# Four conditioning column groups computed beside the key and value stage instead of the gates stage

## The reference

```python
m_lat = [m[:, None, :] for m in adaln(c, w_ada[l], b_ada[l])]     # silu(c) @ w_ada + b_ada, six chunks of 2048
m_ctx = adaln(c_ctx, w_ada[l], b_ada[l])
hc = modulate(rms_norm(ctx, norm1_g[l]), m_ctx[0], m_ctx[1])
pc = hc @ w_in_l[:, :KV_WIDTH]                                    # KV_WIDTH = 3072
h = modulate(rms_norm(x, norm1_g[l]), m_lat[0], m_lat[1])
p = h @ w_in_l
ka, va, kb, vb = split_kv(p[..., :KV_WIDTH], k_norm_a[l], k_norm_b[l])    # keys: rms-normed per head
qa, qb, ga, gb = split_qg(p[..., KV_WIDTH:], q_norm_a[l], q_norm_b[l])
... # rope on queries and keys, attention a (16 heads, 4 kv heads), attention b (8 differential heads)
x_new = x + m_lat[2] * merge_branches(oa, ob, ga, gb, w_br_a[l], w_br_b[l], w_out[l])
```

## Time and profile before

| | us |
|---|---|
| median of 3 runs | 2924.48 (2924.23 to 2924.76) |
| profiled execution | 2922.52 |
| its span | 2920.7 |
| TensorE busy | 2862.6 |
| VectorE busy | 1964.6 |
| ScalarE busy | 1327.5 |
| mean granted TensorE clock | 0.993 of full speed |

### The profile page before, as it was taken

How to read it: one execution, slowest core, us unless ns; L and a number is a source line. 1 busy time by engine, 2 the same in 40 slices (tenths; PEclk the granted TensorE clock), 3 DMA queues, 4 the chain that set the end, 5 groups by cost and what they waited for, 6 DMA issues and landing times.

```text
span 2920.7 us, 34636 instructions
## 1 busy us (share of the span) xinstructions
PE 2862.6 (98%) x13645; PEld 2367.1 (81%) x13645; DVE 1964.6 (67%) x2525; ACT 1327.5 (45%) x1651; POOL 23.5 (1%) x47
## 2 busy tenths in 40 slices
PE   7999999999999999999999999999999999999999
PEld 7888788888888887788888777788878888888887
DVE  5775599999978667753347877767766655655444
ACT  4445454444444446532334545554444444444333
POOL 2000000000000000000000000000000000000000
PEclk9999999999999999999999999999999999999999
DMA  6444577777778887533346655548756777676554
GB/s 215 144 126 145 165 245 255 250 254 258 252 244 271 271 263 234 171 101 95 93 137 188 187 173 173 174 139 260 234 183 223 224 228 226 220 226 206 190 192 151
DMA packets 299954, 583.23 MB, mean 200 GB/s; under 512 B 18393, under 2 KB 18801, under 8 KB 299152
## 3 DMA queue, kind: packets, MB, share of 16 engines
q1 hardware_dynamic: 297472, 573.06, 61.6%
q0 software_dynamic: 2320, 7.96, 0.9%
HBM read 578.85 MB, written 2.10 MB: 199 GB/s over the span
## 4 chain that ended last, share of the span: by engine, by line
PE 91%; DVE 5%; ACT 2%; issue 1%; DMA 1%; SPq 0%; ACTq 0%; DVEq 0%
PE psum L505 22%; PE psum L508 22%; PE psum L507 22%; PE psum L566 3%; PE psum L568 3%; PE psum L567 3%; PE psum L478 2%; PE psum L2821 2%; PE psum L2819 2%; PE psum L2820 2%; PE psum L480 1%; PE psum L481 1%; PE psum L2847 1%; PE psum L2837 1%; PE psum L527 1%
## 5 line engine op out<-in xcount | busy, mean ns | idle before, releaser
L623 DVE TENSOR_TENSOR w_lo<-w_raw,w_hi 128x1024 fp32r<-128x1024 f32 x720 | 877.5, 1223 | 582.8 <-ACT w_hi L617 578.9
L617 ACT ACTIVATE w_hi<-w_raw 128x1024 fp32r<-128x1024 f32 x720 | 762.7, 1060 | 1038.1 <-PE psum L508 1033.6
L505 PE MATMUL psum<-w_hi,x_split 128*128 128x512 f32 x1984 | 782.6, 394 | 4.3 <-issue 3.1
L508 PE MATMUL psum<-w_hi,x_split 128*128 128x512 f32 x1984 | 775.3, 391 | 0.0
L507 PE MATMUL psum<-w_lo,x_split 128*128 128x512 f32 x1984 | 775.3, 391 | 0.0
L505 PEld LDWEIGHTS psum<-w_hi,x_split 128*128 128x128 f32 x1984 | 374.6, 189 | 81.7 <-issue 5.8
L508 PEld LDWEIGHTS psum<-w_hi,x_split 128*128 128x128 f32 x1984 | 374.3, 189 | 78.9
L507 PEld LDWEIGHTS psum<-w_lo,x_split 128*128 128x128 f32 x1984 | 374.8, 189 | 75.6
L505 PE MATMUL psum<-w_hi,hidden_split 128*128 128x512 f32 x704 | 274.9, 391 | 0.0
L654 DVE SCALAR_TENSOR_TENSOR stat<-w_raw,conditions,stat 128x512 f32<-128x512 f32 x360 | 269.5, 749 | 6.8
L508 PE MATMUL psum<-w_hi,hidden_split 128*128 128x512 f32 x704 | 274.0, 389 | 0.0
(11 more groups left out here) (355 smaller groups left out, 3396.6 us busy)
## 6 DMA issues: line engine op xcount, KB each, us to landing
w_raw<-in_w_in SPq DMA_DIRECT2D x216, 512.0 KB, 3.6
w_raw<-in_w_ada SPq DMA_DIRECT2D x192, 512.0 KB, 4.8
w_raw<-in_w_ffn_up SPq DMA_DIRECT2D x176, 512.0 KB, 4.5
w_raw<-in_w_ffn_down SPq DMA_DIRECT2D x88, 512.0 KB, 5.5
w_raw<-in_w_ff_gate SPq DMA_DIRECT2D x88, 512.0 KB, 4.2
w_raw<-in_w_ff_up SPq DMA_DIRECT2D x88, 512.0 KB, 4.3
w_raw<-in_w_ff_down SPq DMA_DIRECT2D x88, 512.0 KB, 3.7
w_raw<-in_w_out SPq DMA_DIRECT2D x64, 512.0 KB, 4.5
```

Of the source, the lines that this page charges most:

```text
L505: nc.tensor.matmul(to, x_hi[:, tokens], hi, start=u == 0 and t == 0, stop=False, skip_group_check=True)
L508: mm = nc.tensor.matmul(to, x_lo[:, tokens], hi, start=False, stop=end and t == 1, skip_group_check=True)
L617: nc.scalar.activation(w_hi[:, b.slot(n)], raw[:, b.raw_slot(k)], ACT.Copy).then_inc(w_rounded, 1)
L623: nc.vector.tensor_tensor(w_lo[:, slot], raw[:, b.raw_slot(k)], r(w_hi[:, slot]), ALU.subtract).then_inc(w_split, 1)
```

## The change

The key and value stage gets conditioning column groups 8 to 11, the gates stage none. A new parameter `lead` puts the first conditioning unit that many units later: with four column groups in 48 units, lead 8 and spare 4, one conditioning unit follows each of units 12 to 43, so VectorE does them in steps 8 to 39. `kv_stream` now calls `ada_turn`, which falls behind units 18, 26, 34 and 42, the third unit of a column group. Bank 6 is shared with the key transposes, so the turn waits for k_out of the keys turned so far, and the key transposes wait for the conditioning group turned before them to be evacuated. The computed values stay as they are.

```diff
-    def __init__(self, Us, ada_cols=(), spare=0, order=None):
+    def __init__(self, Us, ada_cols=(), spare=0, order=None, lead=0):
...
-            while a < 8 * ada and (i - RING + 1) * 8 * ada >= (a + 1) * (n - RING - spare):
+            while a < 8 * ada and (i - RING + 1 - lead) * 8 * ada >= (a + 1) * (n - RING - spare - lead):
...
-    "kv": Phase([8] * 6),
+    "kv": Phase([8] * 6, (8, 9, 10, 11), 4, lead=8),
     "q": Phase([8] * 6),
-    "gates": Phase([8] * 8, (8, 9, 10, 11), 4),
+    "gates": Phase([8] * 8),
...
                 chunks(n, range(4))
+                if n - 3 in b.done:
+                    turned = sum(n > 8 * g + 12 for g in K_GROUPS)
+                    if turned:
+                        pe.wait_ge(S("k_out"), 4 * turned)
+                ada_turn(pe, b, n)
                 late(j, u)
...
                     pe.wait_ge(S("k_roped"), i + 1)
+                    kv = PHASES["kv"]
+                    pe.wait_ge(ada_evacuated, 1 + kv.ada0 + sum(at + 3 <= 8 * j + u for at in kv.done))
                     if i > 0:
                         pe.wait_ge(S("k_out"), 4 * i)
```

## The result

The changed kernel takes 2935.6 us in the median of six runs, the kernel before 2923.9 us in six: a ratio of 1.0042, with a 95% interval of 1.0032 to 1.0051. It is slower by 11.7 us, where 18.5 were forecast. The time lies inside the range of 2933 to 2951 us.

What follows compares the result with a forecast made beforehand. TensorE, busy 2862.6 of 2920.7 us, was taken as the bound. Key stalls 2.2 + 9.9 + 9.9, clock 2 x 3.0, less 9.5 from the gates stage gave +18.5 us: 2943 us, range 2933 to 2951.

Steps and rivals of the forecast that it cites:

- the hold: Key and value stage, steps 24 and 32: VectorE waits for the previous conditioning group's turn, key work queued behind; 9.9 us twice.
- Rival 1: Key and value stage: VectorE is not held, the stage costs 6.4 us; -3.1 us, 2921 us; 5 in 100.
- rival 5: Behind the hold a load lands too late for TensorE, another 3 to 5 us each; about 2950 us; 6 in 100.
- The first key group: Key group 0, turned behind unit 12: conditioning units ahead on VectorE delay its keys; TensorE stalls 2.2 us.
- The clock: Behind both long key stalls TensorE drops to half clock; 3.0 us a stall, between 0 and 4.4.
- Rival 2: Key and value stage: the clock stays high, stalls of 9.9 us cost only themselves; +12.5, 2937 us; 10 in 100.
- Rival 3: Behind the key stalls transposes hold the clock down, 4.4 us a stall; +21.3, 2946 us; 22 in 100.
- as at 1233.96: Kernel before: after 5.06 us idle with only eight transposes, 5.28 us ran at half clock, costing 2.6 us.
- The gates stage: With conditioning work gone, TensorE's stalls there shrink: 9.5 us back, bounds 4.7 and 10.5.
- Rival 4: Gates stage gives back only half, 4.7 us, the softmax chain being late by itself; +23.3, 2948 us; 12 in 100.
- the softmax chain: Gates stage: score, maximum, exponential, probability; claimed to stay and hold the rest of 10.5 us after 9.5 come back.
- the seven stalls: Gates stage: seven larger TensorE stalls before its p-transposes, each said to have conditioning work shortly ahead on VectorE.

Runs made afterwards that it cites:

- e1: Changed kernel with conditioning groups 1 and 3 of the key and value stage summed into a second, free tile; 2916.0 us, 0.9977 of the kernel before.
- e6: Changed kernel with conditioning units four steps earlier (lead 4, spare 8; steps 4 to 35); 2916.2 us, 0.9976 of the kernel before.
- e2: Changed kernel with the key transposes one unit later, behind the sixth unit instead of the fifth; 2923.0 us, 1.0001 of the kernel before.
- e3: Changed kernel with both a second sum tile and the key transposes one unit later; 2908.6 us, 0.9953 of the kernel before.
- e5: Kernel before the change with a second sum tile in the gates stage for its conditioning groups 1 and 3; 2917.0 us, 0.9979 of the kernel before.
- e7: Changed kernel with conditioning units four steps earlier and key transposes one unit later, one sum tile; 2912.8 us, 0.9965 of the kernel before.
- e4: Changed kernel with conditioning column groups 8 to 11 computed in no stage, their columns set to zero; 2907.4 us, 0.9947 of the kernel before.
- e8: Changed kernel with 40 unused matmuls on TensorE ahead of the second and third wait for the keys; 2932.1 us, 1.0032 of the kernel before.

## Why the prediction was right, and where it was off

**The mechanism and its size held.** With T the start of the first part behind the hold (1379.87), the keys were counted for T+20.6 and came at T+20.5 (1400.36); TensorE was counted ready at T+10.7 and was at T+10.6. The stalls were 9.9 and 9.9 us as forecast. e1 shows that the hold is the cause, e6 that its place is what counts, e2 that the keys' time is set by the turn. Rival 1 (VectorE is not held) fell, and so did rival 5: behind the stalls TensorE waits for no weights, so no load came too late for it.

**The first key group** was counted with 2.2 us and cost 1.9 (its row before the transposes: 1.75 us of idle time). Set against TensorE's matmuls, its keys came 2.0 us later than before. The rest is slack, of which the prediction said that there is none: before, the transposes began 0.19 us after the keys were finished, and behind the stall 0.06 us after.

**The clock** was the term with the largest error in this stage: 3.0 us a stall, measured 2.4. Rival 2 (it stays high) fell: both stalls have a stretch at 0.50. Rival 3 (transposes hold it down, then the matmuls as at 1233.96) put 4.4 on it and fell too: 16 transposes and three matmuls stood behind the stall, and the level was back after 4.9 us, no later than the 5.3 us of a stretch with matmuls alone. In e2 it was back 3.5 and 2.7 us after the first transpose of the two groups, with hardly anything but transposes on TensorE until then. In none of these four places did transposes hold the clock down. The Trainium skill, page TensorE: Matmul & The Clock Gate, section Part 4: PE-mode transpose, states that a transpose does not count as busy in the way a matmul does; these four places show no sign of it.

**The gates stage** was counted at 9.5 us of stalls and gave back all 10.5: it is 12.7 us shorter, and four turns are worth about 2.2 of that, if a turn costs there what it costs in the key and value stage. I had counted 1.7 for the turns; the key and value stage with four turns and no stall takes 280.3 us in e3 and without them 278.1 in e5, both with 3.4 us of the lower clock at the start. Rival 4 (half comes back) fell. The 1.0 us that I had left to the softmax chain itself was not there; a recorded idle time of 0.2 us is what remains. The prediction also read the seven stalls too strongly: ahead of the one at 1718.58, VectorE's last conditioning unit had ended at 1713.4, with 1.27 us of idle time since. That stall went too, in e5 already.

**The sum.** By the stages of the two profiles, 2.0 us of the error of 5.8 lie in the key and value stage: 1.1 the clock behind the stalls, 0.3 the first group, 1.1 a shorter stretch at the lower clock at the stage's start (3.4 us instead of 6.8), less 0.5 for the dearer turns. In the gates stage lie 1.5 (1.0 of stalls, 0.5 of turns), and 2.3 in stages that the change does not touch. There the granted clock is 0.50 for 3.4 us in one execution and for 6.8 in another at the same place: in the branch stage 6.8 us before, in e1, e5 and e7, and 3.4 after and in e2, e3, e4, e6 and e8, with about 147.1 and 145.4 us for the stage. It costs 1.6 us, and I take it for chance of the execution, as no edit orders the kernels so. No kernel was profiled twice, but the executions of the kernel before, which is one program, also differ in their clock: 2919.7 us at a mean granted clock of 0.994, 2924.8 us at 0.992. The term that was most off among those the change has is the clock's.

**Luck.** The measured time lies 6.8 us under the forecast by the distances from the kernel before (11.7 and 18.5), right at the lower end that the prediction works out (+11.5, 2936 us), so most of the errors added up on one side. The time by itself fits rival 2 (the clock stays high: +12.5, 2937 us) better than the forecast. That the clock did fall, and that smaller differences elsewhere hid its cost, is told by the traces alone.

## What to carry to other kernels

When work is moved into a stage with idle engines, look not only at how much of it there is but at which of its instructions waits, and what is queued behind that one in program order. Here 46 us of work (32 x 1.45) fitted into VectorE's idle time at a price of 1.9 us in three places (e1), and the wait ahead of two of its groups cost 16 us more and the clock 5. A second buffer for the accumulated sum takes the wait away (e1); other places for the group borders leave it, but where nothing urgent is queued behind it (e6). Moving the consumer by one unit takes what is left (e3, e7).

## What the runs showed of the hardware

A stall of TensorE of 4.5 us (e2) came with 3.4 us at half clock, one of 1.9 us (e1) and one of 3.0 us (before, at 1838) with none. Behind a stall of 9.9 us the half clock lasted 4.9 us after work resumed, no longer than behind the 5.06 us with only eight transposes in them in the kernel before (5.3). Matmuls on data at hand in the idle time (e8) kept the level, and the transposes behind them ran at full speed (1.96 us for 16 instead of 3.68). Keeping the engine busy was worth 2.4 us a stall in the trace, though the work is useless.
